# Router logits computed token-major inside the row-transposition loop of a mixture-of-experts stage, group counts moved ahead of the last row blocks, combine weights as a high and a low part

## The chip, the cores and the metric

The kernel runs on one core of one Trainium2 chip. The metric is the device time of one execution in microseconds (us), the median of several runs. The engines are TensorE (PE in the profile, its weight loads PEld), VectorE (DVE), ScalarE (ACT), GpSimd (POOL) and SyncE (SP), which only issues transfers here.

## The reference, cut to what matters

Two transformer blocks run one after the other on 512 tokens of 1024 features (the second one on 528, with 16 meta tokens in front). The change lies in the first block's second half, a mixture of 16 experts in 4 groups:

```python
grp_prob = softmax(hf @ w_group + b_group);  p_g, g_idx = top_k(grp_prob, 1)
exp_logits = (hf @ w_router + b_router).reshape(-1, 4, 4)
top_vals, e_idx = top_k(exp_logits[t, g_idx], 2)
weights = p_g * softmax(top_vals)            # combine[t, 16], two entries not zero
y = sum_e (silu(hf @ w_gate[e]) * (hf @ w_up[e]) * combine[:, e]) @ w_down[e]
```

Each token goes to one group of four experts, and within it gets two experts' weights.

## The kernel before, in words

Each engine has its own program, written out by hand in a fixed order. The engines meet through semaphores. PSUM is used as a ring of four slots (`PsumWalk`): TensorE claims group g, which waits until group g-4 is released by its reader, writes it and marks it made; readers `arrive` at it and `release` it. Before the change, most large products are three single-pass products of operands split into a high and a low float32r part (line 707).

The stage around the change goes like this. `out_projection` ends the mixer. `norm(SEQ)` sums squares with one-column matmuls (L782) and spreads the inverse root (L767). VectorE makes the eight tiles of h (`Hf[:, k, :]`, L2095), 128 features by 512 tokens each, and ScalarE adds the shift (L1831), which raises `h2_ready` once for each k.

TensorE then does, in order: the router product, feature-major, one float32 matmul for each k with the 20 router columns as the stationary operand and 512 tokens moving (L1164); the transposes of row block 0 (`rows_of_h(0)`, eight 128x128 transposes, L1171); after ScalarE has copied the 20x512 logits to `rrow`, four small transposes to token-major (L1179); the transposes of row blocks 1, 2 and 3 (L1171). Row block 3 needs the PSUM slot of row block 0. Then it waits for the group choice (`gsel_ready`) and counts tokens by group: a prefix over the tokens with a triangle and ones as stationary operands (L1188, L1191) and the totals (L1194).

ScalarE takes each row block out as `TMH` (rounded, L1844). VectorE takes the difference as `TML` (L2600, `rows_lo(t)`, two halves a block), which releases the slot. VectorE's order is: bias and logits to `rl` (L2619), the group choice (five small instructions, L2611 to L2615, raising `gsel_ready`), `rows_lo(0)`, totals and positions (L2629 to L2636), the four permutation tiles `perm` (L2638), `rows_lo(1)` to `rows_lo(3)`, the schedule of the expert blocks (`sched`, L2644 to L2656, on which SyncE waits for the next expert weights), and the choice of the two experts.

TensorE needs all of `TMH`, `TML` and `perm` for the sorting product (L1206), 64 matmuls that put the tokens in the order of their groups. Then come the transposes of `perm` (L1211), the product of `perm` with the combine weights `cmb` (L1217, float32, 16 columns moving), which VectorE copies to `wtab` (L2715), and then 28 units of expert work (L1240, L1249, L1262), whose weights SyncE loads into six chunks. The combine weights are made by ten small VectorE instructions after the third `XSL` copy (L2686 to L2695). After the units the rows are put back (L1282), and the second block follows.

Of the kernel before, what the change touches and what calls it, by code (L numbers as in the profile page):

```python
# [22 lines left out]
F32 = mybir.dt.float32  # L23
F32R = mybir.dt.float32r
ALU = mybir.AluOpType
# [3 lines left out]
P = 128  # L29
D = 1024  # L30
SQ_OWN = 3
KT = D // P
SEQ = 512
META = 16
TALL = SEQ + META
NTOK = SEQ // P
# [122 lines left out]
def build(nc, a, one_hot, out):  # L159
    with ExitStack() as ctx:  # L160
# [10 lines left out]
        PS = ctx.enter_context(nc.psum_tensor("PS", [P, SLOTS, 2, 512], F32))  # L171
# [8 lines left out]
        Hf = at("Hf", B, [KT, TALL]); B += KT * TALL * 4  # L180
# [4 lines left out]
        ident = at("ident", B, [P]); B += 512  # L185
# [6 lines left out]
        w_route = at("w_route", B, [KT, 20]); B += 640  # L192
# [112 lines left out]
        perm = ar("perm", 32768, [NTOK, SEQ], F32R)  # L305
# [8 lines left out]
        m_aT = ar("m_aT", 34816, [2, P])  # L314
        YSH = hf("YSH", KT * TALL * 4, [NTOK, D], F32R)
        YSL = [ar(f"YSL{j}", off, [D], F32R) for j, off in enumerate((36864, 65536, 73216, 49152))]
        rrow = ar("rrow", 65536, [SEQ])
        iota = ar("iota", 67584, [SEQ])
        rl = ar("rl", 69632, [NTOK, 20])
        rt = ar("rt", 69952, [16, NTOK, 4])  # L320
        rp = ar("rp", 70976, [NTOK, 16])
        cmb = ar("cmb", 71232, [NTOK, 16])
        wtab = ar("wtab", 71488, [NTOK * 16])
        rq = ar("rq", 71744, [8, 24])
        sched = ar("sched", 72512, [3, 8], mybir.dt.int32)
        triS = ar("triS", 72704, [P])
# [366 lines left out]
        def _(pe):  # L693
            W = PsumWalk(pe, ready, free)
# [463 lines left out]

            norm(SEQ)

            s = W.claim()
            for k in range(KT):
                pe.wait_ge(h2_ready, k + 1)
                ins = mm(PS[0:20, s, 0, :], w_route[:, k, :], Hf[:, k, 0:SEQ], start=k == 0, stop=k == KT - 1)  # L1164
            W.made(ins)

            def rows_of_h(t):

                s = W.claim()
                for k in range(KT):  # L1170
                    ins = nc.tensor.transpose(PS[:, s, k // 4, P * (k % 4):P * (k % 4) + P], Hf[:, k, P * t:P * t + P], ident[:, :])  # L1171
                W.made(ins)

            route = W.g - 1
            rows_of_h(0)
            W.wait_released(route)
            s = W.claim()
            for t in range(NTOK):
                ins = nc.tensor.transpose(PS[:, s, 0, 20 * t:20 * t + 20], rrow[0:20, P * t:P * t + P], ident[0:20, 0:20])  # L1179
            W.made(ins)  # L1180
            for t in range(1, NTOK):
                rows_of_h(t)

            pe.wait_ge(gsel_ready, 1)
            pe.wait_ge(iota_ready, 2)
# [8 lines left out]
                ins = mm(PS[:, s, 1, 0:4], ones[:, :], gsel[:, t, :], start=t == 0, stop=t == NTOK - 1, skip_group_check=True)  # L1194
            W.made(ins)

            pe.wait_ge(perm_ready, NTOK)
            pe.wait_ge(tmh_ready, NTOK)
            W.wait_released(route + 1)
            for t in range(1, NTOK):  # L1200
                W.wait_released(route + 2 + t)
            for k in range(KT):
                for rows in (TMH, TML):
                    s = W.claim()
# [9 lines left out]
            s = W.claim()  # L1214
            for j in range(NTOK):
                for t in range(NTOK):
                    ins = mm(PS[:, s, 0, 16 * j:16 * j + 16], perm[:, t, P * j:P * j + P].bitcast(F32), cmb[:, t, :],  # L1217
                             start=j == 0 and t == 0, stop=t == NTOK - 1, skip_group_check=True)
            W.made(ins)
            for b in range(1, 5):  # L1220
                W.wait_released(W.g - b)
# [232 lines left out]
        def _(act):  # L1454
# [378 lines left out]
            def expert_hi(c):  # L1833
                x = c % M_SLOTS
                act.wait_ge(m_landed[x], 32 * (c // M_SLOTS + 1))
                af(m_hi[x][:, :], m_raw[x][:, :], ACT.Copy).then_inc(m_hi_done, 1)  # L1836

            evac(rrow[0:20, :], src=lambda s: PS[0:20, s, 0, :])
            for t in range(NTOK):
                if t == 1:  # L1840
                    W.skip(1)
                s = W.arrive()
                W.skip(1)
                af(TMH[:, t, :, :].rearrange("p k (m a) -> p m a k", a=16),  # L1844
                   PS[:, s, :, :].rearrange("p b (m a k) -> p (b m) a k", a=16, k=KT), ACT.Copy).then_inc(tmh_ready, 1)
            expert_hi(0)
            expert_hi(1)
            W.skip(1)
            for k in range(KT):
                s = W.arrive()  # L1850
                ins = af(XSH[:, :, k, :], PS[:, s, 0, :].rearrange("p (j n) -> p j n", j=NTOK), ACT.Copy)
# [199 lines left out]
        def _(dve):  # L2051
# [532 lines left out]
            def r(n, a_=0, b_=4):  # L2584
                return rt[:, n, :, a_:b_]
# [2 lines left out]
                return ap.to_broadcast([P, NTOK, 4])  # L2588

            g0 = W.g  # L2590
            rows_at = [g0 + 1] + [g0 + 2 + t for t in range(1, NTOK)]

            def rows_lo(t):
                W.g = rows_at[t]
# [14 lines left out]
            def first_largest(dst, src, top, below, tmp):  # L2609
# [4 lines left out]
                L(v_.tensor_reduce(r(2, 0, 1), tmp, AX, ALU.max))  # L2614
                return tt(dst, tmp, bc(r(2, 0, 1)), ALU.is_equal)  # L2615

            W.g = g0 + 2
# [3 lines left out]
            W.wait_released(g0 + 2)  # L2621
# [5 lines left out]
            W.g = g0 + 3 + NTOK - 1  # L2627
# [5 lines left out]
            after_pos = W.g  # L2633
            W.wait_released(after_pos - 1)
# [40 lines left out]
            for k in range(KT):  # L2675
                W.skip(1)
                s = W.arrive()
                ins = v_.tensor_copy(XSL[:, :, k, :], PS[:, s, 0, :].rearrange("p (j n) -> p j n", j=NTOK))
                W.release(ins)
                W.wait_released(W.g - 1)  # L2680
                dve.sem_inc(xs_lo, 1)
                if k == 0:
                    expert_lo(0)
                if k == 2:
                    dve.wait_ge(ex_done, 1)
                    L(v_.tensor_reduce(r(11, 0, 1), r(0), AX, ALU.add))  # L2686
                    L(v_.reciprocal(r(11, 1, 2), r(11, 0, 1)))
                    L(ts(r(12, 0, 1), r(15, 0, 1), 1.0, None, ALU.add))
                    L(v_.reciprocal(r(12, 1, 2), r(12, 0, 1)))
                    L(tt(r(12, 2, 3), r(12, 1, 2), r(11, 1, 2), ALU.mult))  # L2690
                    L(tt(r(12, 3, 4), r(12, 2, 3), r(15, 0, 1), ALU.mult))
                    L(tt(r(13), r(8), bc(r(12, 2, 3)), ALU.mult))
                    L(tt(r(14), r(10), bc(r(12, 3, 4)), ALU.mult))
                    L(tt(r(13), r(13), r(14), ALU.add))
                    L(tt(cmb[:, :, :].rearrange("p t (g e) -> p t g e", g=4), r(3).unsqueeze(3).to_broadcast([P, NTOK, 4, 4]),  # L2695
                         r(13).unsqueeze(2).to_broadcast([P, NTOK, 4, 4]), ALU.mult))
                    dve.sem_inc(cmb_ready, 1)
                if k == 4:
                    expert_lo(1)
# [275 lines left out]
```

## Time and profile before

| what | value |
|---|---|
| median of 3 runs | 2263.25 us (2261.7 to 2265.18) |
| profiled execution, its own time | 2266.08 us |
| its span | 2264.3 us |
| granted TensorE clock over the span, mean | 0.945 of full speed |
| TensorE busy | 2125.7 us (94%) |
| VectorE, ScalarE, GpSimd busy | 997.0, 713.2, 622.8 us |
| expert units, first to last matmul | from 702.79 us to about 966 us |

Times inside a table of rows are us from the span's start. A float32 matmul stands in the trace as two records (two weight loads and two matmuls), a float32 transpose and a float32r matmul as one. The granted clock is 1.0 at 2.4 GHz and 0.50 at 1.2 GHz.

### The profile page before, as it was taken

To read this page: it belongs to the slowest core of one execution; us is meant where nothing else is said; L and a number is where in the kernel's file an instruction comes from. 1 tells how busy PE (TensorE), PEld (TensorE's weight loads), DVE (VectorE), ACT (ScalarE), POOL (GpSimd) and SP (SyncE) were. 2 spreads that over 40 slices of the span, in tenths; PEclk is the share of its full clock that TensorE was granted. 3 is DMA by queue.
4 is the path that set the end of the run, shared out by engine and by line. 5 is a ranking of instruction groups with operands and counts; after the bars stand their busy time and mean duration, and the time that the engine had idled before them with its cause. 6 is when DMAs were issued, how large, how long until landed. Compare 5 with 4: busy or idle time off the path is not lost.

```text
span 2264.3 us, 28491 instructions
## 1 busy us (share of the span) xinstructions
PE 2125.7 (94%) x11738; PEld 1773.0 (78%) x11738; DVE 997.0 (44%) x1501; ACT 713.2 (31%) x883; POOL 622.8 (28%) x152
## 2 busy tenths in 40 slices
PE   6699999999979999979999998899999979999997
PEld 6488787888757666669999998788788768888886
DVE  4375577775546656543322236331332243223224
ACT  2542245222235455432121122343232232221222
POOL 0323132443300000023434442221244414444440
PEclk6799999999979999989999998899999979999998
DMA  7121312655216999712222221111123212222220
GB/s 234 39 75 56 94 57 66 197 183 186 75 37 234 344 342 335 267 62 88 93 93 93 91 80 52 56 57 57 56 93 93 75 38 92 95 99 99 96 93 38
DMA packets 175178, 261.04 MB, mean 115 GB/s; under 512 B 12169, under 2 KB 140858, under 8 KB 175086
## 3 DMA queue, kind: packets, MB, share of 16 engines
q1 hardware_dynamic: 173550, 257.65, 34.3%
q10 hardware_dynamic: 1536, 2.10, 0.3%
q8 instruction: 66, 1.08, 0.2%
q14 instruction: 26, 0.21, 0.0%
HBM read 257.62 MB, written 2.11 MB: 115 GB/s over the span
## 4 chain that ended last, share of the span: by engine, by line
PE 88%; DVE 6%; ACT 2%; DMA 1%; issue 1%; SPq 0%; POOL 0%; DVEq 0%; ACTq 0%
PE PS L707 67%; PE PS L1240 6%; PE PS L1262 4%; DVE Hf L2095 2%; PE PS L1394 1%; DVE Hf L2076 1%; DMA m_raw<-in_w_exp_up 1%; PE PS L767 1%; PE PS L1282 1%; PE PS L1206 1%; DVE R L2107 1%; PE PS L813 1%; PE PS L782 1%; PE PS L1346 1%; PE PS L922 0%
## 5 line engine op out<-in xcount | busy, mean ns | idle before, releaser
L667 POOL TENSOR_TENSOR w_lo<-w_raw,w_hi 128x2048 fp32r<-128x2048 f32 x133 | 618.2, 4649 | 1544.9 <-ACT w_hi L1513 1544.9
L707 PE MATMUL PS<-HH,w_hi 128*128 128x512 f32 (+1 forms) x1936 | 602.4, 349 | 46.1 <-DVE HL L2069 26.9
L707 PE MATMUL PS<-HL,w_hi 128*128 128x512 f32 (+1 forms) x1936 | 599.9, 348 | 0.0
L707 PE MATMUL PS<-HH,w_lo 128*128 128x512 f32 (+1 forms) x1936 | 597.0, 346 | 0.0
L1513 ACT ACTIVATE w_hi<-w_raw 128x2048 fp32r<-128x2048 f32 x133 | 254.6, 1915 | 716.6 <-DMA w_raw<-in_w_ffn_in 299.3
L707 PEld LDWEIGHTS PS<-HH,w_hi 128*128 128x128 f32 x1936 | 339.4, 191 | 99.1 <-issue 50.4
L707 PEld LDWEIGHTS PS<-HH,w_lo 128*128 128x128 f32 x1936 | 338.6, 191 | 45.7
L707 PEld LDWEIGHTS PS<-HL,w_hi 128*128 128x128 f32 x1936 | 338.9, 191 | 44.7
L2779 DVE TENSOR_TENSOR actf<-PS,sg 128x528 f32<-128x528 f32 (+1 forms) x44 | 30.8, 699 | 420.2 <-PE PS L707 420.2
L2790 DVE TENSOR_TENSOR yacc<-yacc,PS 128x528 f32<-128x528 f32 (+1 forms) x176 | 122.2, 695 | 104.6 <-PE PS L707 104.4
L2672 DVE TENSOR_TENSOR m_lo<-m_raw,m_hi 128x2048 fp32r<-128x2048 f32 x56 | 128.3, 2292 | 77.9 <-ACT m_hi L1836 77.3
L707 PE MATMUL PS<-ah,w_hi 128*128 128x264 f32 (+1 forms) x528 | 141.0, 321 | 0.0
L707 PE MATMUL PS<-al,w_hi 128*128 128x264 f32 (+1 forms) x528 | 140.8, 321 | 0.0
L707 PE MATMUL PS<-ah,w_lo 128*128 128x264 f32 (+1 forms) x528 | 140.5, 320 | 0.0
L1836 ACT ACTIVATE m_hi<-m_raw 128x2048 fp32r<-128x2048 f32 x56 | 107.1, 1916 | 90.7 <-DMA m_raw<-in_w_exp_up 90.7
L1262 PE MATMUL PS<-m_raw,m_aT 128*128 128x512 f32 x224 | 101.2, 594 | 2.5 <-ACT m_aT L1881 2.5
L1240 PE MATMUL PS<-m_hi,XBH 128*128 128x512 f32 x224 | 101.6, 454 | 0.4 <-DVE wtab L2715 0.4
L707 PEld LDWEIGHTS PS<-ah,w_hi 128*128 128x128 f32 x528 | 87.5, 188 | 7.9
L707 PEld LDWEIGHTS PS<-al,w_hi 128*128 128x128 f32 x528 | 87.4, 188 | 7.9
L707 PEld LDWEIGHTS PS<-ah,w_lo 128*128 128x128 f32 x528 | 87.3, 188 | 7.9
L1240 PE MATMUL PS<-m_hi,XBL 128*128 128x512 f32 x224 | 88.7, 396 | 0.0
L1240 PE MATMUL PS<-m_lo,XBH 128*128 128x512 f32 x224 | 88.4, 395 | 0.0
(427 smaller groups left out, 2618.2 us busy)
## 6 DMA issues: line engine op xcount, KB each, us to landing
w_raw<-in_w_in SPq DMA_DIRECT2D x49, 1024.0 KB, 5.1
w_raw<-in_w_ffn_in SPq DMA_DIRECT2D x44, 1024.0 KB, 4.9
m_raw<-in_w_exp_gate SPq DMA_DIRECT2D x56, 512.0 KB, 4.3
m_raw<-in_w_exp_up SPq DMA_DIRECT2D x56, 512.0 KB, 5.8
m_raw<-in_w_exp_down SPq DMA_DIRECT2D x56, 512.0 KB, 4.9
w_raw<-in_w_ffn_out SPq DMA_DIRECT2D x22, 1024.0 KB, 4.8
mod_late<-in_w_mod SPq DMA_DIRECT2D x16, 1024.0 KB, 5.2
w_raw<-in_w_out SPq DMA_DIRECT2D x8, 1024.0 KB, 4.9
```

The source lines that it names most:

```text
L667: pool.tensor_tensor(w_lo[:, s, :], w_raw[:, s, :], w_hi[:, s, :].bitcast(F32), ALU.subtract).then_inc(split, 1)
L707: ins = mm(o, l, r, **k)
L767: ins = mm(PS[:, s, bank, col:col + G], rsc[0:G, c0 + j:c0 + j + 1].to_broadcast([G, P]), ident[0:G, 0:G], start=True, stop=True)
L782: ins = mm(PS[0:G, s, 0, j:j + 1], sq[:, k, G * j:G * j + G], ones[:, 0:1], start=k == 0 and j == 0, stop=k == last, skip_group_check=True)
L1240: ins = mm(PS[:, 0, u % 2, :].rearrange("p (g f) -> p g f", g=2), l[:, blk % 2, kk, :], r[:, :, k, :], start=kk == 0 and n == 0, stop=kk = ...
L1262: ins = mm(PS[:, 2 + blk % 2, b, :], m_aT[:, k, :], w[:, k, 512 * b:512 * b + 512], start=ee == 0 and k == 0, stop=ee == N_GRP - 1 and k == 1)
L1513: af(w_hi[:, c % RING, :], w_raw[:, c % RING, :], ACT.Copy).then_inc(hi_done, 1)
L1836: af(m_hi[x][:, :], m_raw[x][:, :], ACT.Copy).then_inc(m_hi_done, 1)
L2095: ins = stt(sv(Hf[:, k, 0:T], T), sv(src(k), T), gain(k), ps(s, T), ALU.mult, ALU.mult)
L2672: tt(m_lo[x][:, :], m_raw[x][:, :], m_hi[x][:, :].bitcast(F32), ALU.subtract).then_inc(m_lo_dve, 1)
L2779: W.release(tt(sv(f, T), ps(s, T), sv(sg[:, m, 0:T], T), ALU.mult))
L2790: W.release(tt(y, y, ps(s, T), ALU.add))
```

## The change

The router product is turned round: for each k and each of the four blocks of 128 tokens, the 128x128 block of h is the stationary operand and the 20 router columns move, so that the logits come out with tokens on the partitions. In the same loop over k the transposes of row blocks 0 and 1 are issued, into two further slots that are claimed ahead. `rrow`, its copy and the four small transposes go away. The group counts are issued behind these, and row blocks 2 and 3 come after the counts. The product with the combine weights takes `cmb` as a high and a low float32r part, which VectorE makes with two more instructions.

```diff
-            s = W.claim()
+            route = W.g
+            first = []
+            for x in range(3):
+                first.append(W.claim())
+                W.g += 1
+            W.g = route
             for k in range(KT):
                 pe.wait_ge(h2_ready, k + 1)
-                ins = mm(PS[0:20, s, 0, :], w_route[:, k, :], Hf[:, k, 0:SEQ], start=k == 0, stop=k == KT - 1)
-            W.made(ins)
-            route = W.g - 1
-            rows_of_h(0)
-            W.wait_released(route)
-            s = W.claim()
-            for t in range(NTOK):
-                ins = nc.tensor.transpose(PS[:, s, 0, 20 * t:20 * t + 20], rrow[0:20, P * t:P * t + P], ident[0:20, 0:20])
-            W.made(ins)
-            for t in range(1, NTOK):
-                rows_of_h(t)
+                for t in range(NTOK):
+                    choice = mm(PS[:, first[0], 0, 20 * t:20 * t + 20], Hf[:, k, P * t:P * t + P], w_route[:, k, :],
+                                start=k == 0 and t == 0, stop=k == KT - 1, skip_group_check=True)
+                rows = [row_of_h(first[1 + t], t, k) for t in range(2)]
+            W.made(choice)
+            W.made(rows[0])
+            W.made(rows[1])
             pe.wait_ge(gsel_ready, 1)
             pe.wait_ge(iota_ready, 2)
...
             W.made(ins)
+            for t in range(2, NTOK):
+                s = W.claim()
+                for k in range(KT):
+                    ins = row_of_h(s, t, k)
+                W.made(ins)
             pe.wait_ge(perm_ready, NTOK)
             pe.wait_ge(tmh_ready, NTOK)
...
             for j in range(NTOK):
                 for t in range(NTOK):
-                    ins = mm(PS[:, s, 0, 16 * j:16 * j + 16], perm[:, t, P * j:P * j + P].bitcast(F32), cmb[:, t, :],
-                             start=j == 0 and t == 0, stop=t == NTOK - 1, skip_group_check=True)
+                    for n, part in enumerate((cmb_hi, cmb_lo)):
+                        ins = mm(PS[:, s, 0, 16 * j:16 * j + 16], perm[:, t, P * j:P * j + P], part[:, t, :],
+                                 start=j == 0 and t == 0 and n == 0, stop=t == NTOK - 1 and n == 1, skip_group_check=True)
...
-            evac(rrow[0:20, :], src=lambda s: PS[0:20, s, 0, :])
...
+                    L(v_.tensor_copy(cmb_hi[:, :, :], cmb[:, :, :]))
+                    L(tt(cmb_lo[:, :, :], cmb[:, :, :], cmb_hi[:, :, :].bitcast(F32), ALU.subtract))
                     dve.sem_inc(cmb_ready, 1)
```

`row_of_h(s, t, k)` is one transpose of `rows_of_h`. VectorE's order stays as it was; only the numbers of the groups at which it arrives are new, and ScalarE's likewise.

## Rows read from the trace of the kernel before

**Rows 1.** The page: head, busy time, share of the chain by engine

```profile
span 2264.3 us, 28491 instructions
...
PE 2125.7 (94%) x11738; PEld 1773.0 (78%) x11738; DVE 997.0 (44%) x1501; ACT 713.2 (31%) x883; POOL 622.8 (28%) x152
...
PE 88%; DVE 6%; ACT 2%; DMA 1%; issue 1%; SPq 0%; POOL 0%; DVEq 0%; ACTq 0%
```

**Rows 2.** Windows in the expert units: stretch, busy by engine, clock, DMA share, GB/s

```profile
760.00:800.00 40.00, 40.00 (x151) 27.21 (x150) 24.75 (x16) 21.30 (x20) 0.00 (x0) 1.00 0.98 344
```

**Rows 3.** The chain of waits, 648 to 678 us: start, us, what

```profile
648.95 9.83 PE PS L1164 x16
658.79 1.02 PE PS L1171 x8
659.81 0.36 PE PS L1179 x4
...
660.27 0.25 DVE rl L2619
...
662.14 1.95 DVE TML L2600 x2
664.08 0.04 issue
664.13 1.31 PE PS L1171 x8
665.43 0.24 PE PS L1188 x2
665.67 1.26 PE PS L1191 x6
666.93 1.72 PE PS L1194 x8
...
671.57 5.53 DVE TML L2600 x6
```

**Rows 4.** The timeline, 639 to 703 us: start, us, instruction, idle time before

```profile
645.19 2.08 PE L767 MATMUL PS<-ident,rsc 128*128 128x128 f32 x8 [0.57 <-DVE rsc L2089]
...
658.71 0.86 PEld L1171 LDWEIGHTS PS<-ident,Hf 128*128 128x128 f32 x8 [0.85 <-issue]
...
659.85 5.46 ACT L1844 ACTIVATE TMH<-PS 128x1024 fp32r<-128x1024 f32 x3 [0.44 <-PE PS L1171]
...
668.68 0.16 DVE L2629 COPY rq<-PS 128x4 f32<-128x4 f32 x1 [4.61 <-PE PS L1194]
...
677.34 2.04 PE L1206 MATMUL PS<-perm,TMH 128*128 128x512 f32 x4 [8.70 <-DVE TML L2600]
...
688.79 0.23 DVE L2695 TENSOR_TENSOR cmb<-rt 128x64 f32<-128x64 f32 x1
```

**Rows 5.** One line in windows (L813; L1217 in two; L782): PE, PEld, clock

```profile
32.30:39.10 6.80, 6.80 (x32) 6.80 (x32) 0.50 0.00 0
...
697.13:698.90 1.77, 1.77 (x16) 1.77 (x17) 1.00 0.81 245
699.10:702.00 2.90, 2.90 (x15) 2.90 (x15) 0.50 0.46 179
...
639.50:641.90 2.40, 2.40 (x24) 2.40 (x23) 1.00 0.11 15
```

**Rows 6.** Windows of all engines, columns as in rows 2

```profile
649.00:654.60 5.60, 5.60 (x7) 1.00 (x8) 3.74 (x7) 4.42 (x7) 0.00 (x0) 0.50 0.00 1
654.70:658.70 4.00, 4.00 (x10) 0.80 (x8) 0.00 (x0) 0.00 (x0) 0.00 (x0) 1.00 0.02 4
677.30:681.90 4.60, 4.56 (x11) 3.62 (x12) 3.72 (x23) 0.60 (x1) 0.00 (x0) 0.50 0.18 38
...
214.40:221.10 6.70, 6.70 (x20) 5.33 (x20) 3.59 (x7) 2.40 (x2) 3.14 (x1) 0.50 0.00 0
```

**Rows 7.** The line of the group totals by itself: records, duration min/median/max in ns

```profile
L1194 PEld LDWEIGHTS PS<-rt,ones x8: 333/333/333, 666.7 to 668.2; 128*128 128x128 f32 x8
L1194 PE MATMUL PS<-rt,ones x8: 354/354/354, 666.8 to 668.3; 128*128 128x4 f32 x8
```

More of the change, by code:

```diff
@@ L316, in build @@
         YSL = [ar(f"YSL{j}", off, [D], F32R) for j, off in enumerate((36864, 65536, 73216, 49152))]
-        rrow = ar("rrow", 65536, [SEQ])
         iota = ar("iota", 67584, [SEQ])
@@ L323, in build @@
         wtab = ar("wtab", 71488, [NTOK * 16])
+        cmb_hi = ar("cmb_hi", 73216, [NTOK, 16], F32R)
+        cmb_lo = ar("cmb_lo", 73472, [NTOK, 16], F32R)
         rq = ar("rq", 71744, [8, 24])
@@ L1159, in _, with row_of_h @@
             norm(SEQ)
-            s = W.claim()
+            def row_of_h(s, t, k):
+                return nc.tensor.transpose(PS[:, s, k // 4, P * (k % 4):P * (k % 4) + P], Hf[:, k, P * t:P * t + P], ident[:, :])
+            route = W.g
[4 more added lines that the diff above has]
+            W.g = route
             for k in range(KT):
                 pe.wait_ge(h2_ready, k + 1)
-                ins = mm(PS[0:20, s, 0, :], w_route[:, k, :], Hf[:, k, 0:SEQ], start=k == 0, stop=k == KT - 1)
-            W.made(ins)
-            def rows_of_h(t):
-                s = W.claim()
-                for k in range(KT):
-                    ins = nc.tensor.transpose(PS[:, s, k // 4, P * (k % 4):P * (k % 4) + P], Hf[:, k, P * t:P * t + P], ident[:, :])
-                W.made(ins)
-            route = W.g - 1
-            rows_of_h(0)
-            W.wait_released(route)
-            s = W.claim()
-            for t in range(NTOK):
-                ins = nc.tensor.transpose(PS[:, s, 0, 20 * t:20 * t + 20], rrow[0:20, P * t:P * t + P], ident[0:20, 0:20])
-            W.made(ins)
-            for t in range(1, NTOK):
-                rows_of_h(t)
+                for t in range(NTOK):
[5 more added lines that the diff above has]
+            W.made(rows[1])
+            rows_group = [route + 1, route + 2, route + 4, route + 5]
             pe.wait_ge(gsel_ready, 1)
@@ L1195, in _ @@
             W.made(ins)
+            for t in range(2, NTOK):
[3 more added lines that the diff above has]
+                W.made(ins)
             pe.wait_ge(perm_ready, NTOK)
             pe.wait_ge(tmh_ready, NTOK)
-            W.wait_released(route + 1)
-            for t in range(1, NTOK):
-                W.wait_released(route + 2 + t)
+            for g in rows_group:
+                W.wait_released(g)
             for k in range(KT):
@@ L1836, in expert_hi @@
                 af(m_hi[x][:, :], m_raw[x][:, :], ACT.Copy).then_inc(m_hi_done, 1)
-            evac(rrow[0:20, :], src=lambda s: PS[0:20, s, 0, :])
-            for t in range(NTOK):
-                if t == 1:
-                    W.skip(1)
+            g0 = W.g
+            for t, g in enumerate((g0 + 1, g0 + 2, g0 + 4, g0 + 5)):
+                W.g = g
                 s = W.arrive()
-                W.skip(1)
                 af(TMH[:, t, :, :].rearrange("p k (m a) -> p m a k", a=16),
                    PS[:, s, :, :].rearrange("p b (m a k) -> p (b m) a k", a=16, k=KT), ACT.Copy).then_inc(tmh_ready, 1)
+            W.g = g0 + 6
             expert_hi(0)
             expert_hi(1)
-            W.skip(1)
             for k in range(KT):
@@ L2590, in _ @@
             g0 = W.g
-            rows_at = [g0 + 1] + [g0 + 2 + t for t in range(1, NTOK)]
+            rows_at = [g0 + 1, g0 + 2, g0 + 4, g0 + 5]
             def rows_lo(t):
@@ L2615, in first_largest @@
                 return tt(dst, tmp, bc(r(2, 0, 1)), ALU.is_equal)
-            W.g = g0 + 2
+            W.g = g0
             s = W.arrive()
@@ L2620, in _ @@
                          b_route[:, 0:20].unsqueeze(1).to_broadcast([P, NTOK, 20]), ALU.add))
-            W.wait_released(g0 + 2)
+            W.wait_released(g0)
             L(first_largest(r(3), rl[:, :, 0:4], r(1, 0, 1), r(0), r(4)))
@@ L2626, in _ @@
             tot, incl, off = rq[:, 1, 0:4], rq[:, 2, 0:4], rq[:, 3, 0:4]
-            W.g = g0 + 3 + NTOK - 1
+            W.g = g0 + 3
             s = W.arrive()
@@ L2632, in _ @@
             W.release(tt(r(5), PS[:, s, 0, 0:16].rearrange("p (t g) -> p t g", g=4), off.unsqueeze(1).to_broadcast([P, NTOK, 4]), ALU.add))
-            after_pos = W.g
-            W.wait_released(after_pos - 1)
+            after_pos = g0 + 6
+            W.wait_released(g0 + 3)
             L(tt(r(5), r(5), r(3), ALU.mult))
```

## The prediction

> **What bounds the kernel now.** I read the page first, then the windows, then the chain of waits and the timeline around the change. By the page TensorE is busy 94% of the span and holds 88% of the chain [rows 1]. In the expert units, which follow the changed stage, it is busy without a gap at the full clock, while the transfers run at a 0.98 share [rows 2]. Both are near their limit there, so the units neither wait for an earlier start nor absorb a later one. What the change does to the time is therefore the shift of the moment at which the units begin, and that depends on when the sorting product (L1206) begins. Everything between L1206 and the units is made of the same instructions in the same order, but for two small ones.
>
> The chain through the router stage reads like this [rows 3]. The router product takes 9.83 us, row block 0 takes 1.02, the four logit transposes 0.36, so the token-major logits are there at 660.17. VectorE then needs 1.3 us to the group choice. The counts don't follow at once: TensorE stands in front of row block 3, whose PSUM slot is free only when VectorE has finished the first `TML` (662.14 to 664.08). It transposes until 665.43 and counts until 668.65. VectorE had stood idle 4.61 us for that [rows 4]. Then come positions, `perm` and three `TML` blocks, 8.45 us in all to the last one's end at 677.10, and TensorE, idle for 8.70 us, starts L1206 at 677.34 [rows 3, 4].
>
> **Part 1, the router loop.** It loses 16 records of L1164, 8 transposes that stood behind them, 4 small ones, and ScalarE's copy. It gets 8 x (4 float32 matmuls of 2 records + 2 transposes) = 80 records, each with a full 128x128 weight load. What a record costs depends on the clock. At 0.50, 32 records of one moving column take 6.80 us, 0.213 each; 15 records of 16 columns fall into 2.90 us, 0.193 to 0.21 each by how the edges count. At 1.00 they take 0.111 (16 in 1.77) and 0.100 to 0.12 (24 in 2.40) [rows 5]; eight transposes issue in 0.86 us, 0.108 each [rows 4]. So the number of records counts here and not their columns, and 20 columns fit in. For transposes at 0.50 the nearest row is L767 with 128 columns, where eight records take 2.08 us, and without the last one's own length 0.234 each [rows 4]; the 16 transposes would then add 0.3 us.
>
> Which clock applies? The loop starts at 0.50, as L1164 does now [rows 6], because nothing ahead of it is changed. L1164, which streams 512 columns a record, had brought the clock up by 654.7 [rows 6]. The loop replaces these by short ones. In two places the trace shows short matmuls issued without a gap: 6.8 us of L813 stay at 0.50, and under L1217 the clock fell from 1.00 to 0.50 while TensorE was never idle, and stayed there [rows 5]. Two transposes in ten records stream 128 columns, which is more than L813 has and less than L1164. I take 0.50 for the whole loop.
>
> The last logit matmul is the 78th record (two transposes come behind it). With the first at about 649.1 it ends at 649.1 + 77 x 0.213 + 0.354 (its own length [rows 7]) = 665.9. Before, the logits were there at 660.17. **Term 1: +5.7 us.**
>
> The Trainium skill (TensorE: Matmul & The Clock Gate, Part 1) says that the default state is throttled and sustained matmul activity releases it, which read plainly would bring this gapless loop to the full clock; the sum would then be that of rival A below. L813's row speaks against taking any busy stretch as such activity.
>
> **Part 2, the counts ahead of row blocks 2 and 3.** The group choice takes the same 1.3 us and is there at 667.2. TensorE has nothing in front of the counts: 16 records, at 0.50, make 0.3 + 15 x 0.213 + 0.354, about 3.8 us with the hand-over, so the totals are there at 671.05. From logits to totals that is 5.15 us; before it was 668.65 - 660.17 = 8.48. **Term 2: -3.3 us.** What goes is the wait for the first `TML` and the transposes of row block 3 (1.31 us).
>
> The cover for what was moved: VectorE's first `TML` starts 2.3 us behind ScalarE's first `TMH`, as now (659.85 to 662.14 [rows 3, 4]), so 666.15 + 2.3 + 1.95 = 670.4, before the totals. Row blocks 2 and 3 cost 16 x 0.213 and end at 672.9 and 674.6; ScalarE's copies (1.94 us each) end at 674.9 and 676.8; VectorE wants them at 675.8 and 677.65, since positions and `perm` (2.9 us) and `TML` 1 stand in front. Slack is 0.9 us each. The slot of row block 3 is that of row block 0, free at 670.4. So the stretch behind the totals keeps its 8.45 us: **term 3: 0**, and L1206 starts at 679.7. ScalarE's two weight copies `m_hi`, which stand behind the last `TMH`, end at 680.5, and the first sorted group comes at 681.8; covered by 1.2 us. If row block 3 were late, its lateness would go straight to L1206. The schedule stays behind the last `TML`, so SyncE's wait and the loads that follow keep their distance to L1206.
>
> **Part 3, the combine weights.** TensorE has 16 float32 matmuls of 2 records before and 32 float32r matmuls of one record after: 32 full weight loads either way, so nothing changes there (a float32r load on the same tile was never seen with 16 columns; L1206 only shows it under 512). VectorE gets two instructions of the size of L2695 (0.23 us [rows 4]), some 0.45 with the links. They stand between two `XSL` copies that free PSUM slots for L1206. Bounds are 0 (slots in hand) and 0.45; I take 0.2. **Term 4: +0.2.**
>
> **Sum.** 5.7 - 3.3 + 0 + 0.2 = +2.6 us. The profiled execution took 2266.08 us, so its like would take 2268.7; it lies 2.8 above the median of the runs, so the median goes from 2263.25 to 2265.9. A measurement of this kernel tells about 0.2%, 4.5 us, from no change, so this is "the same", leaning to slower.
>
> **Rivals.**
>
> *A, the clock rises in the loop as it does now.* Low until 654.65, that is 26 records; 52 more at 0.118 and 0.27 for the end give 661.1. Choice at 662.4, counts warm in 2.3 us at 664.7, first `TML` over at 665.5, which now decides: 3.2 us ahead of 668.68. With term 4 it is -3.0: 2260.3. For it: gapless issue, and transposes in the mix. Against: rows 5. If L1206 too then began at the full clock, half of its 4.6 us at 0.50 [rows 6] would go as well: 2258.0, which is faster.
>
> *B, each record costs its full length.* This is the other side. If the loads of alternating stationary operands and destinations (token block, row block, logits) didn't overlap the matmul before, a record would take 0.354 in place of 0.213 [rows 7]: 77 x 0.141 = 10.8 more, 2276.7. It decides slower once a record takes more than 0.213 + (4.5 - 2.6) / 77 = 0.238. For it: L767's 0.234. Against: L1188 to L1194, with changing operands, hold the 0.213 (14 records in 2.98 us [rows 3]).
>
> *C, the clock comes later behind the stage.* L1206 resumes low and stayed so for 4.6 us; the rise after 214.4 took up to 6.7 [rows 6]. Starting 2.4 us later it may miss its rise, here and at the first unit. Half of 2.1 at one place and up to half that again at the other make some +1.6: 2267.5.
>
> *D, L1206 alone begins at the full clock*, since TensorE's idle time in front of it shrinks from 8.7 to about 5 us: -2.3, 2263.6.
>
> **Chances and range.** The sum as it stands 0.72 (same 0.64, slower 0.08); A 0.08 (same 0.05, faster 0.03); B 0.05 (slower); C 0.12 (same 0.06, slower 0.06); D 0.03 (same). So faster 0.03, same 0.78, slower 0.19. The range takes in A's single form, C and the 0.45 and 0.3 bounds with the spread of the runs shown (some 2 us each way), and leaves out B: 2259.5 to 2269.5.
>
> **What would show it.** In the new trace: the loop's 80 records over some 17 us with the clock at 0.50 (right) or about 12 us with a rise in it (A) or over 19 us (B); the first bias instruction L2619 near 666; counts straight behind the group choice; no idle time of VectorE at the later `TML` blocks; L1206 at about 679.7; first unit near 705.4; 32 records for the combine product in some 5 us. The prediction is wrong if the loop's clock is not 0.50, if `TMH` 3 comes late to VectorE, or if the clock behind the stage goes another way.

## The result, and the profile after

The changed kernel took 2271.05 us in the median of 20 runs (2264.25 to 2275.24), the kernel before 2265.86 us in the median of 20 runs beside them (2260.49 to 2270.24). The ratio is 1.0021, with a 95% interval of 1.0011 to 1.0030: slower by some 4.8 us. The forecast was 2265.9 us and "the same, leaning to slower". The way was right, but the measured median lies above the range of 2259.5 to 2269.5 us. Two things add up. The difference was put at +2.6 us and is larger, and the base from which it was counted, the 2263.25 us of the first three runs, lay 2.6 us under what 20 runs give. Two repetitions of the changed kernel (below) gave 1.0012 and 1.0017, so the three together say about 1.0017, or 3.8 us.

The page of the profiled execution (its own time 2266.41 us, one of the fastest of the 20), lines as in [rows 1]:

```profile
span 2264.7 us, 28594 instructions
...
PE 2129.3 (94%) x11782; PEld 1784.0 (79%) x11782; DVE 993.9 (44%) x1503; ACT 712.9 (31%) x882; POOL 623.8 (28%) x152
...
PE 89%; DVE 6%; ACT 2%; issue 1%; DMA 1%; SPq 0%; POOL 0%; DVEq 0%; ACTq 0%
```

The span looks the same as before, because this execution came to the router stage 3.3 us earlier (645.67 against 648.95) for reasons that lie ahead of the change. So all that follows is counted from the first router matmul. The chain of waits in the changed stage (start, us, what), to hold against [rows 3]:

```profile
645.67 1.87 PE PS L1174 x8
...
660.20 1.54 PE PS L1174 x8
...
661.83 0.25 DVE rl L2620
...
663.23 0.61 PE PS L1186 x2
663.84 1.26 PE PS L1189 x6
665.10 1.72 PE PS L1192 x8
...
669.73 1.17 DVE TML L2601
670.91 0.86 issue
671.77 1.15 DVE TML L2601 x2
672.92 0.74 issue
673.66 2.08 DVE TML L2601 x2
...
675.98 18.12 PE PS L1208 x64
```

and the timeline of the same stretch, to hold against [rows 4]:

```profile
647.37 0.67 PE L1163 MATMUL PS<-ident,Hf 128*128 128x128 f32 x2
647.83 1.73 PE L1174 MATMUL PS<-w_route,Hf 128*128 128x20 f32 x8
...
649.86 1.73 PE L1174 MATMUL PS<-w_route,Hf 128*128 128x20 f32 x8
...
666.67 3.65 PE L1163 MATMUL PS<-ident,Hf 128*128 128x128 f32 x16
675.98 2.05 PE L1208 MATMUL PS<-perm,TMH 128*128 128x512 f32 x4 [5.66 <-DVE TML L2601]
...
669.65 6.08 DVE L2601 TENSOR_TENSOR TML<-PS,TMH 128x512 fp32r<-128x512 f32 x6
...
687.65 0.20 DVE L2698 CAST cmb_hi<-cmb 128x64 fp32r<-128x64 f32 x1
687.88 0.23 DVE L2699 TENSOR_TENSOR cmb_lo<-cmb,cmb_hi 128x64 fp32r<-128x64 f32 x1
...
668.65 4.21 ACT L1845 ACTIVATE TMH<-PS 128x1024 fp32r<-128x1024 f32 x2 [2.96 <-PE PS L1163]
```

What to see: the loop runs at 2.03 us a step (649.86 less 647.83), the counts (L1186 to L1192) follow straight on the group choice, and the sorting product, now L1208, starts 30.31 us behind the first router matmul. It was 28.38. The windows, columns as in [rows 2], show the clock in the loop, at the sorting product's start and at the first unit's:

```profile
645.70:661.80 16.10, 16.10 (x79) 16.10 (x80) 3.76 (x7) 4.44 (x7) 0.00 (x0) 0.50 0.01 2
675.90:682.10 6.20, 6.12 (x15) 4.81 (x16) 5.01 (x25) 1.65 (x3) 0.00 (x0) 0.50 0.42 126
701.30:706.00 4.70, 4.70 (x11) 3.73 (x12) 4.46 (x2) 1.14 (x1) 0.00 (x0) 0.50 0.00 0
```

TensorE is busy without a gap for 16.1 us and stays at 0.50 for all of it. The sorting product too is low for 6.1 us (4.6 in [rows 6]) and the first unit for 4.7. In the other five profiles of the changed kernel these are 3.5 to 6.2 and 4.2 to 5.5 us, in the five of the kernel before 4.4 to 4.6 and 3.0 to 3.4.

### The profile page after: what moved, and what is told of

Read it like the earlier page. It is cut to its first block, busy times and chain, and to the rows that moved or that the text cites. A ratio compares the mean times of both kernels' runs of the same rounds, so it can differ in the third digit from the quotient of the medians.

```text
span 2264.7 us, 28594 instructions
## 1 busy us (share of the span) xinstructions
PE 2129.3 (94%) x11782; PEld 1784.0 (79%) x11782; DVE 993.9 (44%) x1503; ACT 712.9 (31%) x882; POOL 623.8 (28%) x152
## 4 chain that ended last, share of the span: by engine, by line
PE 89%; DVE 6%; ACT 2%; issue 1%; DMA 1%; SPq 0%; POOL 0%; DVEq 0%; ACTq 0%
PE PS L708 67%; PE PS L1243 6%; PE PS L1265 4%; DVE Hf L2096 2%; PE PS L1397 1%; DVE Hf L2077 1%; PE PS L768 1%; PE PS L1208 1%; PE PS L1285 1%; DVE R L2108 1%; PE PS L814 1%; DMA m_raw<-in_w_exp_up 1%; PE PS L1174 1%; PE PS L783 1%; PE PS L1349 1%
```

## The experiments

All ratios are against the kernel before, run on the same chips, with the 95% interval in brackets. Times of a stage are counted from the first router matmul: "logits" is the start of the bias instruction on VectorE, "totals" the copy of the group totals, "sort" the first matmul of the sorting product, "unit" the first of the expert units, and "units" the length from there to the first put-back matmul (L1282). They are read off the timeline of each kernel's own trace:

| kernel | logits | totals | sort | unit | units | ratio |
|---|---|---|---|---|---|---|
| before | 11.31 | 19.72 | 28.38 | 53.84 | 267.1 | |
| before again | 11.21 | 19.72 | 28.38 | 53.24 | 266.2 | 1.0003 |
| changed | 16.16 | 21.17 | 30.31 | 55.61 | 268.7 | 1.0021 |
| changed again | 16.16 | 21.17 | 30.26 | 55.57 | 270.2 | 1.0012 |
| changed, third | 16.16 | 21.17 | 30.39 | 55.68 | 270.9 | 1.0017 |
| counts ahead alone | 11.19 | 14.93 | 23.71 | 48.54 | 269.9 | 0.9982 |
| the same again | 11.37 | 15.11 | 23.88 | 48.76 | 268.7 | 0.9993 |
| counts back | 16.16 | 22.48 | 31.19 | 57.28 | 266.0 | 1.0021 |
| warm | 13.33 | 18.33 | 27.44 | 52.76 | 268.7 | 1.0011 |
| combine alone | 11.37 | 19.72 | 28.38 | 53.72 | 269.1 | 0.9999 |
| logits first | 13.92 | 20.55 | 29.59 | 54.95 | 268.1 | 1.0016 |
| loop twice | 32.38 | 37.38 | 46.47 | 71.78 | 268.2 | 1.0093 |
| keep warm | 8.51 | 12.24 | 21.01 | 45.85 | 267.2 | 0.9979 |
| warm sort | 8.61 | 12.34 | 21.22 | 46.05 | 268.9 | 0.9973 |

Each row but its ratio is one profiled execution. Counted like this, a stage leaves out what delays the first router matmul itself. From the last matmul of `out_projection` to it there are 9.8 to 10.6 us in all kernels but two: 13.9 in warm, which has twenty matmuls in front of it, and 12.7 in warm sort.

**Counts ahead alone.** Part 2 without the rest, put into the kernel before:

```diff
             W.made(ins)
-            for t in range(1, NTOK):
-                rows_of_h(t)
+            rows_of_h(1)
...
             W.made(ins)
+            rows_of_h(2)
+            rows_of_h(3)
```

> The kernel before with part 2 alone: the wide router product, its copy and the four small transposes stay, row block 1 follows, then the counts, then row blocks 2 and 3; combine product as before. If the sum's term 2 is right, the logits come as before (11.2 us behind the first router matmul), the totals some 5.2 to 5.5 us behind them in place of 8.5, and the sorting product starts some 3 us earlier, 25.2 us behind the first router matmul in place of 28.4: about -3 us in the median, ratio 0.9987. If moving the counts gives nothing (row blocks 2 and 3 late in their place), ratio 1.000 and VectorE idles 2 to 3 us at the later TML blocks.

> Counts ahead alone, a second time on other chips: its stage was 5.0 us shorter than that of the kernel before, so ratio 0.9978 if the stage passes one to one to the end (0.9982 was measured), and 1.000 if the first measurement was chance. The totals again 3.7 us behind the logits, since the counts run at the full clock there.

ScalarE's and VectorE's group numbers follow. The ratio was 0.9982 (0.9971 to 0.9994) and the second time 0.9993 (0.9983 to 1.0002), whose interval just takes in no gain. The logits come as before, the totals 3.74 us behind them in place of 8.41, and the sort 4.7 us earlier. That is more than the 3 expected, because the clock, which rose under the wide router product, is still at 1.00 when the counts come. The timeline of the first one:

```profile
663.96 0.40 PE L1187 MATMUL PS<-rt,triS 128*128 128x16 f32 x2 [0.48 <-DVEq L2622]
664.20 0.81 PE L1190 MATMUL PS<-rt,ones 128*128 128x12 f32 x6
664.87 1.03 PE L1193 MATMUL PS<-rt,ones 128*128 128x4 f32 x8
...
675.09 2.05 PE L1206 MATMUL PS<-perm,TMH 128*128 128x512 f32 x4 [5.49 <-DVE TML L2599]
```

The 14 records of L1190 and L1193 take 1.70 us (664.20 to 665.90), against 2.98 in [rows 3]. So the wide router product leaves TensorE at the full clock for what comes next. The gain of 4.8 us at the first unit arrives only in part at the end (about 2.8 by the mean of the two ratios); the units' stretch is 2 to 3 us longer than the 266.9 us that five profiles of the kernel before have in the mean (below).

**Counts back.** The changed kernel with part 2 undone:

```diff
+            for t in range(2, NTOK):
+                s = W.claim()
+                for k in range(KT):
+                    ins = row_of_h(s, t, k)
+                W.made(ins)
             pe.wait_ge(gsel_ready, 1)
...
-            for t in range(2, NTOK):
-                s = W.claim()
-                for k in range(KT):
-                    ins = row_of_h(s, t, k)
-                W.made(ins)
```

> The changed kernel with part 2 undone: row blocks 2 and 3 before the counts again. If the loop is what costs (term 1) and the counts what gives (term 2), the totals come some 8 us behind the logits, the sorting product starts about 3 us later than in the changed kernel, 33.3 us behind the first router matmul: +5 us against the kernel before, ratio 1.0022, or 1.0035 if the changed kernel's own 1.0021 is taken as it was measured. If the counts' place doesn't matter, the ratio is the changed kernel's.

The ratio was 1.0021 (1.0011 to 1.0031). The stage got 1.7 us longer than in the changed kernel at the first unit, not 3: the clock had risen when the counts came, so that they ran fast. Timeline (TensorE waits for the first `TML` again) and window:

```profile
669.35 0.37 PE L1191 MATMUL PS<-rt,triS 128*128 128x16 f32 x2 [0.91 <-DVE TML L2601]
669.56 0.81 PE L1194 MATMUL PS<-rt,ones 128*128 128x12 f32 x6
...
668.00:670.00 2.00, 1.09 (x10) 0.89 (x9) 1.20 (x2) 2.00 (x2) 0.00 (x0) 1.00 0.00 0
```

The clock rose at 668 us, some 3.2 us into a run of eighteen transposes. That such a run brings it up is not shown: sixteen in a row (666.67 in the changed kernel's timeline above, and in logits first) stayed at 0.50. By its ratio counts back can't be told from the changed kernel; the traces tell them apart.

**Warm.** The clock as the loop's price, tested by matmuls that compute nothing that is used:

```diff
             W.g = route
+            for x in range(20):
+                mm(PS[:, first[0], 1, :], HH[:, x % KT, 0:P], HH[:, x % KT, 0:SEQ], start=True, stop=True)
             for k in range(KT):
```

> The changed kernel with 20 matmuls of 512 columns into an unused half of the claimed slot, ahead of the router loop (they compute nothing that is used). They take some 7 us, of which 1.6 lie in an idle gap. If the low clock is what makes the loop dear, its ten records a step take 1.0 to 1.2 us in place of 2.03 for as long as the clock stays up, 8 to 10 us for the loop if it stays up to the end, and the logits come about where they came without the 20 matmuls or 1 to 2 us earlier. If a record's price is not the clock's, the steps stay at 2.0 us and everything behind comes 5 us later. If short matmuls let the clock fall again within the loop, the steps go from about 1.1 to 2.0 us partway.

The third case came true. Windows of the fillers, of the loop's first steps and of its rest:

```profile
651.40:656.70 5.30, 5.30 (x22) 4.32 (x21) 4.97 (x8) 4.19 (x7) 0.00 (x0) 0.86 0.17 67
656.80:659.70 2.90, 2.90 (x30) 2.90 (x28) 0.36 (x2) 1.04 (x2) 0.00 (x0) 1.00 0.00 0
660.20:669.80 9.60, 9.60 (x49) 9.60 (x49) 0.00 (x0) 0.00 (x0) 0.00 (x0) 0.50 0.00 0
```

Thirty records in 2.90 us, 0.097 each, at 1.00; then 49 in 9.60 us, 0.196 each, at 0.50, with no idle time between. The same records cost twice as much, so the price is the clock's, and it is in the loop that the clock is lost. The ratio was 1.0011 (1.0000 to 1.0023), no different from the changed kernel's: the twenty matmuls also delay the first router matmul by some 4 us.

**Changed again, and before again.** Both unaltered.

> The changed kernel unaltered, to place its measured +0.21% against the other kernels on the same chip and to get a second profile. If the stage is the whole of it, the sorting product starts 30.3 us behind the first router matmul and the first expert unit some 55.5 behind (28.4 and 53.8 before), and the ratio is near 1.001; if something behind the stage adds to it, the ratio is near 1.002 again and the profile shows it between the first unit and the end.

> The changed kernel unaltered a third time, to narrow what is measured against the 2.0 us that its stage shows: ratio 1.0009 if the stage is all of it, 1.0021 if the first measurement stands; the profile's first router matmul to first unit 55.6 us again.

> The kernel before, unaltered, as a measure of what this comparison tells and for a second profile of its stage. Ratio 1.000 within 0.1%. If the stage of the first profile was a typical one, first router matmul to first expert unit is again 53.8 us to within 1; if the moment at which the clock rises under the router product moves from run to run, the logits come anywhere from 10 to 13 us behind the first matmul, and the units' stretch (267.1 in the first profile; 266.0 to 270.2 in the five others) varies without any cause in the stage.

The changed kernel gave 1.0012 (1.0002 to 1.0022) and 1.0017 (1.0008 to 1.0026), the kernel before against itself 1.0003 (0.9991 to 1.0014). The stage repeats to 0.1 us up to the totals and to 0.6 at the first unit. The units' stretch doesn't.

**Combine alone.** The kernel before with part 3, the diff as in the change.

> The kernel before with part 3 alone: combine weights as a high and a low part. If term 4 (+0.2) is right, ratio 1.000, the product again 32 records at 0.11 or 0.21 each by the clock, sorting product to first unit 25.5 us as before. If the split product carries what the profile of the changed kernel's stage doesn't explain, ratio 1.0005 or more and that stretch 26 to 27 us.

The ratio was 0.9999 (0.9986 to 1.0011), sort to unit 25.34 us (25.46 and 24.86 in the first two traces of the kernel before). Part 3 costs nothing that can be seen in the stage, nor in the time to within some 3 us. But the units' stretch of its one profile, 269.1 us, is some 2 us longer than the kernel before ever has, with the first unit no later. In the changed kernel 32 records as expected (groups by shape, 16 and 16):

```profile
L1220 PE MATMUL PS<-cmb_lo,perm 128*128 128x16 f32 x16 | 4.0, 276 | 0.0
L1220 PE MATMUL PS<-cmb_hi,perm 128*128 128x16 f32 x16 | 3.9, 269 | 0.4 <-ACT permT L1472 0.4
```

**Logits first.** The transposes of row blocks 0 and 1 behind the loop over k:

```diff
-                rows = [row_of_h(first[1 + t], t, k) for t in range(2)]
             W.made(choice)
-            W.made(rows[0])
-            W.made(rows[1])
+            for t in range(2):
+                for k in range(KT):
+                    ins = row_of_h(first[1 + t], t, k)
+                W.made(ins)
```

> The changed kernel with the 16 transposes of row blocks 0 and 1 taken out of the loop over k and put behind it. If a record costs the same whatever it is, the logits come after 62 x 0.203 + 0.35 = 13.0 us in place of 16.2, the group choice runs beside the transposes, the counts start 1.3 to 2 us later than the choice is ready and the totals come some 1.3 us earlier than in the changed kernel; the sorting product then starts 29 us behind the first router matmul: -1.3 us against the changed kernel, ratio near 1.001. If the loop is paced by something else than its records (the arrival of h, 0.67 us a step), the logits come at 16 us again.

The timeline shows the 64 records alone:

```profile
651.37 13.81 PE L1174 MATMUL PS<-w_route,Hf 128*128 128x20 f32 x64 [1.69 <-ACT Hf L1835]
```

Without the last record's own 0.37 that is 0.213 each; in the mixed loop a step of ten took 2.03, so there the two transposes add 0.32. By their starts they take more (0.46, from 647.37 to 647.83 above), but the second short record behind them follows the first after 0.07 and not 0.21. The logits came 2.2 us earlier than in the changed kernel (not 3.2, since I had taken 0.203 for the short records too), the totals and the first unit 0.6 us earlier (not 1.3), since the counts now stand behind the transposes. The ratio was 1.0016 (1.0005 to 1.0027). The loop is paced by its records, not by the arrival of h.

**Loop twice.** The loop over k run through a second time:

```diff
-            for k in range(KT):
+            for k in list(range(KT)) + list(range(KT)):
```

> The changed kernel with its router loop run through twice (the second pass starts the sums anew, so only 80 further records are added). The loop's records at 0.203 add 16.2 us to the stage. If a delay of the stage passes one to one to the end, the kernel is 16.2 us slower than the changed one and 18 to 20 slower than the kernel before, ratio 1.0080 to 1.0088. If what stands behind the stage makes a delay larger (two and more times, which the changed kernel's 4.8 us for 2.0 us of stage would ask for), the ratio is 1.015 or more; if the expert units absorb part of a delay, it is under 1.0075.

The ratio was 1.0093 (1.0077 to 1.0108), 21.1 us. The stage is 16.2 us longer than the changed one, at 0.50 from end to end (window of both passes):

```profile
652.60:684.90 32.30, 32.17 (x159) 32.20 (x160) 3.92 (x7) 4.59 (x7) 0.00 (x0) 0.50 0.00 1
```

16.2 and the changed kernel's own 3.8 make 20.0, 1.0088, inside the interval. So, to within the interval's 3.5 us either way, a delay of the stage is neither absorbed nor multiplied. What the changed kernel has beyond its stage is a sum of its own, not a factor.

**Keep warm, and warm sort.** Counts ahead alone, with fillers in TensorE's gaps in the norm ahead; the second one with 12 more in front of the sorting product. Their products are used nowhere.

```diff
+            def fill(s, n):
+                for x in range(n):
+                    mm(PS[:, s, 1, :], HH[:, x % KT, 0:P], HH[:, x % KT, 0:SEQ], start=True, stop=True)
...
+                    if k == SQ_OWN:
+                        fill(s, 5)
...
                 W.made(ins)
+                fill(W.claim(), 2)
                 spread_root(T)
+                fill(W.claim(), 7)
...
             rows_of_h(3)
+            W.g += 1
+            fill(W.claim(), 12)
+            W.g -= 1
```

The last three added lines are those of warm sort.

> Counts ahead with the wide router product (the better one of the first four), and 14 matmuls of 512 columns that compute nothing that is used, in the gaps of TensorE in the norm ahead (5 before the last sum of squares, 2 before the root's spread, 7 before the router product). If the low clock is what the router stage pays, the clock stays at 1.00 through them, the router product is paced by h (0.67 us a step) and ends about 6.5 us behind its first matmul in place of 9.8: some -3.5 us more than counts ahead alone, ratio 0.9967. If the one-column and 128-column matmuls between them let the clock fall all the same, the ratio stays at 0.998 or loses a little by delayed norm steps.

> Counts ahead with the wide product and the filled norm gaps, and 12 more matmuls that compute nothing that is used, behind row block 3, where TensorE idles 5.3 us before the sorting product. If the idle time is what leaves the clock low there, the sorting product starts at the full clock (0.23 us a matmul from the first on in place of 0.43 for the first ten or so) and takes 15 to 16 us in place of 17.1; the stage to the first unit gets 1.5 to 2.3 us shorter than with the norm gaps alone (45.85), and the ratio is near 0.997. If the fillers hold the sorting product up, its start moves from 21.0 us behind the first router matmul to later by as much as they overhang.

Keep warm, timeline: the fillers (L798), and the wide router product in 7.03 us in place of 9.83 [rows 3], now at a granted clock of 1.00 throughout:

```profile
649.46 1.97 PE L798 MATMUL PS<-HH 128*128 128x512 f32 x7
651.49 7.03 PE L1187 MATMUL PS<-Hf,w_route 128*20 128x512 f32 x16
```

The ratio was 0.9979 (0.9965 to 0.9992), so of the further 2.7 us at the first unit little shows against counts ahead alone (0.9982 and 0.9993). Warm sort gave 0.9973 (0.9963 to 0.9983), the lowest ratio here, some 6 us under the kernel before. But its own step failed. The fillers in front of the sorting product ran at the full clock, and it had fallen again when the product began 4 us later:

```profile
670.20:673.20 3.00, 3.00 (x15) 2.15 (x13) 3.00 (x6) 3.00 (x2) 0.00 (x0) 1.00 0.00 0
677.20:680.10 2.90, 2.89 (x7) 2.32 (x8) 2.29 (x15) 0.60 (x1) 0.00 (x0) 0.50 0.00 0
```

Its stage, 46.05 us, is that of keep warm, and the two can't be told apart by their intervals.

**Six more profiles, for the units' stretch.** The changed kernel's stage is 2 us longer, its time 3.8. The stretch of the units looked longer too, so both kernels were profiled three more times each, unaltered.

> One look at the kernel before, for the length of the expert units' stretch (first L1240 to first L1282). So far 267.1, 266.2 and 269.1 (combine alone) against 268.7, 270.2 and 270.9 in the changed kernel. If that difference of 2.4 us is the change's, the stretch is 266 to 268 again; if it is chance of late transfers, it comes anywhere in 266 to 271.

> One look at the changed kernel, for the same stretch: 269 to 271 if the difference is the change's, anywhere in 266 to 271 if it is chance. Low clock after the first unit's start some 4 to 5.5 us (3 in the kernel before), since the combine product ends at another point of the clock's fall and rise.

> The same look at the kernel before a second time: 266 to 268 if the difference in the units' stretch is the change's.

> The same look at the changed kernel a second time: 269 to 271 if the difference in the units' stretch is the change's.

> The same look at the kernel before a third time, on other chips: the units' stretch at 266 to 268 if the difference in it is the change's, anywhere in 266 to 271 if it is chance.

> The same look at the changed kernel a third time: 269 to 271 if the difference is the change's, anywhere in 266 to 271 if it is chance.

| from the first router matmul, us | before, 5 profiles | changed, 6 profiles |
|---|---|---|
| to the first unit, mean | 53.5 (53.2 to 53.8) | 55.6 (55.5 to 55.7) |
| units' stretch, mean | 266.9 (266.2 to 267.2) | 269.7 (268.1 to 271.2) |
| to the first put-back matmul, mean | 320.4 (319.4 to 321.0) | 325.3 (323.6 to 326.7) |
| to the end, mean | 1613.9 (1611.7 to 1615.4) | 1617.7 (1615.3 to 1619.0) |

The ranges of the units' stretch don't overlap. So the difference, 2.8 us, belongs to the changed kernel and is hardly chance, and with 2.1 us of stage and 1.1 us that the rest of the kernel takes less it makes the 3.8 us. Here is the first of the new profiles of each kernel, windows of the first 90 us or so from just before the first unit. Before:

```profile
700.44:750.40 49.96, 49.24 (x183) 34.46 (x184) 30.35 (x19) 24.48 (x22) 0.00 (x0) 0.97 0.85 296
750.40:790.40 40.00, 39.75 (x146) 26.09 (x145) 24.88 (x16) 19.38 (x18) 0.00 (x0) 1.00 0.97 340
```

Changed:

```profile
704.01:754.00 49.99, 49.17 (x178) 33.91 (x179) 28.84 (x20) 22.97 (x22) 0.00 (x0) 0.95 0.83 289
754.00:794.00 40.00, 39.12 (x146) 25.93 (x144) 23.91 (x15) 20.27 (x18) 0.00 (x0) 1.00 0.96 333
```

In the first 50 us the changed kernel gets five records less done, and its mean clock is 0.95 and not 0.97: the clock rises later. In the next 40 us TensorE is idle for 0.88 us and not 0.25. Over the whole stretch, in the mean of the profiles, TensorE is busy for 262.2 us and not 260.9, and idle for 7.5 and not 5.9. What it waits for stands in the groups of the whole stretch (the last column: idle before, releaser). Before:

```profile
L1262 PE MATMUL PS<-m_raw,m_aT 128*128 128x512 f32 x224 | 101.2, 594 | 2.0 <-ACT m_aT L1881 1.8
```

Changed:

```profile
L1265 PE MATMUL PS<-m_raw,m_aT 128*128 128x512 f32 x224 | 101.7, 597 | 4.3 <-ACT m_aT L1882 3.6 <-issue 0.6
```

The changed kernel's profile shown here has the longest such wait; over all profiles the wait for `m_aT` is 1.5 to 2.5 us before and 1.7 to 3.6 in the changed kernel. `m_aT` is late because it stands on ScalarE behind a copy `m_hi` of weights that have just landed. The changed kernel shows such a stop in the tenth unit (the chain, then ScalarE's timeline):

```profile
794.13 0.37 issue
794.50 3.67 PE PS L1265 x8
...
792.22 1.92 ACT L1839 ACTIVATE m_hi<-m_raw 128x2048 fp32r<-128x2048 f32 x1 [1.94 <-DMA m_raw<-in_w_exp_up]
794.04 0.37 ACT L1882 ACTIVATE m_aT<-PS 128x256 f32<-128x256 f32 x1
```

This stop, some 90 us behind the first unit, is there in all six profiles of the changed kernel, with 0.4 to 1.8 us of idle time, and in none of the five of the kernel before. Why the weights land late just there is not shown. The traces give a candidate that no run tests: in all six a 16 KB packet of the queue that carries instructions (q8) comes 4.6 to 6.7 us ahead of the stop, 82.5 to 85.8 us behind the first unit. In the kernel before the packet nearest to it comes at 89.6 to 91.8, and no stop follows. Counts back and warm sort have both the early packet and the stop, but logits first has the packet (82.4) and no stop.

What goes with a longer stretch over all twenty profiles is not how far the stage moved, but how long the first unit runs at 0.50. With 2.8 to 3.4 us of it the stretch is 266.0 to 267.2 us: the kernel before five times, counts back (its first unit 3.8 us later) and keep warm (7.6 us earlier). With 4.2 to 5.5 us it is 268.1 to 271.2: twelve profiles, the changed kernel's six among them. The twentieth, combine alone, doesn't fit: 3.3 us and 269.1. A way in which the one could make the other can be read off the first 20 us of the units. There the transfers have room, as this window of the kernel before shows:

```profile
700.49:720.49 20.00, 19.33 (x70) 14.06 (x71) 11.49 (x8) 8.78 (x8) 0.00 (x0) 0.91 0.66 220
```

The first new weights are asked for once the first unit has used its own, 4.5 to 4.8 us behind its start in the kernels with the short low stretch and in combine alone, 5.1 to 5.7 in the others. What is asked for late is hard to make up for afterwards, with transfers at 0.97. No experiment changed the first unit's clock alone, so this is argued, not shown.

## Why the prediction was right or wrong

**The loop (term 1): right in kind, 0.9 too high.** The logits came 16.16 us behind the first router matmul and not 11.31, +4.85 where +5.7 was said. The clock was 0.50 throughout, as taken. The 80 records took 0.203 each in the mix, and not 0.213: a step of ten took 2.03 and not 2.13. The working had expected the transposes to make it dearer, by 0.3 in all.

**The counts (term 2): right.** Logits to totals took 5.01 us and not 8.41: -3.4 where -3.3 was said.

**The stretch behind the totals (term 3): 0 was said, it was +0.5.** Totals to sort took 9.14 us and not 8.66. The six `TML` halves, one unbroken run in both kernels, took 6.08 us where they had taken 5.60:

```profile
671.48 5.60 DVE L2600 TENSOR_TENSOR TML<-PS,TMH 128x512 fp32r<-128x512 f32 x6
```

The slack of 0.9 us that the working gave to row blocks 2 and 3 was there: their `TMH` copies ended 0.9 and 0.8 us before VectorE began on them. What the working put at nothing is that ScalarE's copies now run beside the halves. Before, ScalarE had finished its last one 0.6 us before they began, and each took 1.01 us. Now the first half took 1.27 us beside a `TMH` copy that itself took 2.20 (1.96 before). The run of six takes 5.96 to 6.17 us in all profiles of the changed kernel and in warm, logits first and loop twice, and 5.60 or 5.61 where no copy runs beside it. It takes 5.71 to 5.83 in counts ahead alone, keep warm and warm sort, where `TMH` copies overlap it too; what makes the overlap dearer in the former is not shown.

**The combine weights (term 4): right to the trace's resolution**, 0.2 said; combine alone gave 0.9999.

At the first unit the stage made +2.1 us in the mean of the profiles, where +2.6 was said.

**The step that failed is the one ahead of all terms**: that what the change does to the time is the shift of the moment at which the units begin, since the units "neither wait for an earlier start nor absorb a later one". That put a change of the units' own length at nothing. The shift itself does pass on: in loop twice 16.2 us of delay gave about 17. But the units' stretch became 2.8 us longer in the changed kernel, more than the whole stage's 2.1, and some 2 us longer in counts ahead alone, where the stage's gain of 4.8 us came out as 2.8. The prediction had read [rows 2], no gap in TensorE and transfers at 0.98, as "both near their limit", and took that for indifference. That window begins 57 us behind the first unit; in the first 20 us the transfers are at 0.66, and what is lost there can't be seen in it.

**Rival C** (the clock comes later behind the stage, +1.6, 0.12) was the nearest. In the mean the first unit was low for 4.7 us in the changed kernel and for 3.3 in the kernel before. At half speed that accounts for 0.7 us directly. Waiting is the larger part of the 2.8 us, 1.6, and no rival named it; whether the later clock causes it too stays open, as does the remaining half microsecond. **A** fell with the clock at 0.50 in the loop, **B** with 0.203 a record, **D** with the sorting product's start at 0.50 in every profile of the changed kernel. Warm shows both sides of A: the same loop runs at half the price when the clock is up, and does not hold it.

**The page of the skill.** The prediction weighed the rule of the Trainium skill (TensorE: Matmul & The Clock Gate, Part 1) that sustained activity releases the clock against L813's row, and went by the row. The 16.1 us without a gap at 0.50 agree with the row.

**The base.** The range was laid around 2263.25 us, the median of three runs. Twenty gave 2265.86. A single run of this kernel scatters over 10 us, so half of the distance between 2265.9 and 2271.05 is the base and not the change.

Left open: which part of the change makes the units longer (combine alone has a long stretch too, in one profile); what makes the weights late in the tenth unit of the changed kernel, whose loads and order are untouched; and the 1.1 us that the rest gets back, which lies within what single profiles differ by.

## What to carry to other kernels

A small-matrix product that is turned round so that the large operand is stationary pays for a full weight load a record, and here its short moving side didn't keep TensorE's clock up: 80 short records cost 16 us and left the clock low, where the wide form of the same product took 9.8 us and handed the full clock to what followed. Of a change of several parts, price and time each alone: the reordering by itself was worth some 3 us here, and was hidden under the loss of the other part. A shift of the next stage's start passes on, but that stage's own length can change as well, even where none of its instructions did: compare it in several profiles of both kernels, from its first microseconds on. And where work is moved to run beside another engine's, price what they may cost each other: here that was the 0.5 us that term 3 missed.

## What the runs showed that was not expected

Two transposes put among eight short float32 matmuls at the low clock added 0.32 us to a step, 0.16 each, where sixteen in a row cost 0.21 each (3.65 us with 0.45 for the end); the time is gained at the matmul behind them, and why is not shown. A copy of ScalarE and a subtraction of VectorE that ran side by side took 2.20 and 1.27 us, where they had taken 1.96 and 1.01 apart; in other kernels here the same pair overlapped at hardly any cost. Fourteen matmuls that nobody uses, in the gaps of the norm, took the router product from 9.83 to 7.03 us. Twelve more in front of the sorting product did nothing, since the clock was gone again within 4 us of idle time.
